# PEER routing in another place: heads routed at dots 1, 3 and 5, tile 1's first two heads together in group 7, and a reordered seam with banded pooling

## The chip, the cores and the metric

The kernel runs on one core of a Trainium2 chip. The time is the device time of the core in microseconds, the median of several executions; lower is better. The engines are PE (TensorE, matmuls), DVE (VectorE), ACT (ScalarE), POOL (GpSimd, here only an issuer of indirect gathers) and SP (SyncE, an issuer of plain transfers). Each works through its own list of instructions in order, and they wait for one another by semaphores.

## What is computed

The reference is a two-layer encoder over 256 tokens of width 2048 in float32. Layer 0 mixes with attention and an mLSTM, layer 1 with a multi-scale pooling:

```python
hn = rmsnorm(h, norm_mix_g[layer])
if layer % 2 == 0: h = h + attn_mlstm_mixer(hn, ...)
else:              h = h + multiscale_pool_mixer(hn, pool_w, layer_scale)
h = h + peer_ffn(rmsnorm(h, norm_ffn_g[layer]), peer_wq, peer_keys, peer_u, peer_v)
```

The pooling subtracts each token from the mean over a window of 2, 4, 8 or 16 tokens around it (a window for each of four channel groups), then applies a linear map for each group. Both layers end with a retrieval of experts (PEER, K = 16, 8 heads, 128 keys a side):

```python
q = (xn @ w_query).reshape(b, s, 8, 2, 128)
sc = einsum('bshpc,hpnc->bshpn', q, sub_keys)
s_top, i_top = top_k(sc, 16)                     # for each half of the key
cand = s_top[..., 0, :, None] + s_top[..., 1, None, :]
best, pos = top_k(cand, 16);  expert = i_top0 * 128 + i_top1 at pos
gate = softmax(best)
act = gelu(einsum('tkd,td->tk', u[expert], xt))  # 128 rows of u for each token
y   = einsum('tk,tkd->td', gate * act, v[expert])
```

## The kernel before

Tokens lie on the 128 partitions, in two tiles (t = 0, 1). In each layer the expert stage has 256 *rows*: row n gathers one expert vector of `u` for each of 128 tokens (a tile of 128 x 2048, 1 MB) and multiplies it with the token's normed input. Rows 0 to 127 belong to tile 0 and rows 128 to 255 to tile 1; sixteen rows are one head of one tile, a *group* (j = 0 to 15), and k counts the rows within a group.

*Gathers.* POOL issues them in the order of n (`gather_u`). At the first row of a group it waits for `idx_ready`, that is until DVE has written this group's indices into `idx_all`. Otherwise it waits for a free buffer: `U` has 6 slots for tile 0 (row n may go out when the dot six dots earlier is done), and the rows with n % 4 == 2 from group 1 to group 7 go to a second ring `UX` of 3, whose dot PE computes. For tile 1 `U` has 7 slots, the third row there waits until PE has done all of its dots (`ux_mm`), and the first until all routing is done, for the slots lie over the routing's buffers.

*DVE* runs through the rows: `dot(L, n)` for each row that isn't PE's, `pick` four times a group to read PE's results off a diagonal, and between the dots the routing, in three parts: `route_halves` (the 16 best of 128 scores on each side, with their indices, and the sums of pairs), `route_pairs` (the 16 best of 256), and `route`, which is `route_experts` (the indices, increments `idx_ready`) and `route_gates` (softmax, after an exponential on ACT). Ten *events* a layer go through one bank of PSUM with scores: tile 0 head 0, tile 0 head 1, tile 1 head 0, tile 1 head 1 (each for one tile), and heads 2 to 7 (each for both tiles). PE computes `queries` and `scores` of an event, ACT copies the queries (`route_q`), and `sc_free` keeps the scores of the next event off until DVE has read the last.

*PE* besides turns each `UX` row (`dot_u`: transposes, a copy by ACT in `turn_u`, and matmuls); the first row of a quad waits until the last quad's results are picked.

*SP* loads query weights `wq` into two slots by turns, a head's after PE has used the slot; then the weights of the dense part. Between the layers, at the *seam*, it loads the pooling matrices `PM`, `poolw`, the scale `lsB` (`PM` and `lsB` lie in the second `wq` slot), `wq` of head 0, the keys and the gains; `wq` of head 1 waits until the pooled result is added to `h` (`h1_ready`, 8). PE pools by full 128 x 256 matrices (L1629), though only the tokens within 8 of each other are not zero.

After the dots come the gathers of `v` (half of the width on DVE) and a dense part on PE; the change leaves them alone.

## Time and profile before

| | us |
|---|---|
| median of 3 runs | 3136.72 (3135.51 to 3137.5) |
| profiled execution | 3131.51 |
| its span, first to last instruction | 3129.6 |
| PE / DVE / ACT / POOL busy | 2292.8 / 2180.1 / 677.7 / 1011.0 |
| moved by the transfers | 1059.08 MB, mean 338 GB/s |
| mean granted clock of PE | 0.851 of 2.4 GHz |

The expert stage of layer 0 begins at 523.5 us of the span with the first gather, that of layer 1 at 1848.8. The seam is from 1782 to 1848. A row of a timeline says when an instruction (or a run of equal ones) began and how long it took, and in brackets how long its engine had been idle before it and who ended that. A busy engine that nobody waits for costs nothing, and an idle one costs only where its late work is waited for.

### The profile page before, as it was taken

What the parts mean: (1) busy time and instruction counts of PE and PEld (TensorE: products, weight loads), DVE (VectorE), ACT (ScalarE), POOL (GpSimd) and SP (SyncE); (2) the same over time, 40 slices, a digit from 0 to 9 for tenths busy, and PEclk for the clock granted to TensorE, in tenths of its full rate; (3) what the DMA queues carried; (4) which work ended last, traced back from release to release, by engine and by line L of the source; (5) the groups of instructions that cost most, each with busy time, mean ns of one, the idle gap of its engine ahead of it and who ended that gap; (6) DMA issues with size and microseconds to landing.
All of it is one profiled execution on the core that took longest, in us unless ns stands there. A gap on an engine that the chain in (4) does not pass through costs nothing.

```text
span 3129.6 us, 25966 instructions
## 1 busy us (share of the span) xinstructions
PE 2292.8 (73%) x9248; PEld 1706.4 (55%) x9248; DVE 2180.1 (70%) x3263; ACT 677.7 (22%) x1645; POOL 1011.0 (32%) x1028
## 2 busy tenths in 40 slices
PE   8999999588853400999999575888533109999994
PEld 4685545587743300766666344878533006666662
DVE  1341113988979999856666739889899998566667
ACT  1241111122229910200000011222289203000000
POOL 0000000432333333344544414233333333445444
PEclk9999999799975555999999787999855559999997
DMA  5423243989989999699999948899999996999998
GB/s 212 153 111 135 108 169 152 414 332 404 378 364 422 421 422 413 214 410 409 409 409 409 378 182 334 332 406 380 377 421 421 421 420 209 410 409 409 409 409 337
DMA packets 194528, 1059.08 MB, mean 338 GB/s; under 512 B 21856, under 2 KB 22240, under 8 KB 121312
## 3 DMA queue, kind: packets, MB, share of 16 engines
q0 software_dynamic: 147456, 805.37, 63.7%
q1 hardware_dynamic: 46944, 252.06, 20.3%
q8 instruction: 74, 1.21, 0.2%
q14 instruction: 54, 0.44, 0.0%
HBM read 1055.24 MB, written 2.10 MB: 338 GB/s over the span
## 4 chain that ended last, share of the span: by engine, by line
DMA 48%; PE 23%; DVE 22%; issue 3%; POOL 3%; ACT 1%; DVEq 0%; SPq 0%; ACTq 0%; POOLq 0%
DMA arena<-pu,idx_all 23%; DMA xnT<-pvg,idx_all 13%; DMA arena<-pvg,idx_all 11%; DVE arena L1120 10%; PE bank L1293 6%; DVE h L1146 4%; PE bank L1378 3%; PE bank L1599 2%; PE bank L1607 2%; PE low L1498 2%; PE bank L1533 1%; POOL arena L449 1%; PE low L1487 1%; PE low L1555 1%; PE bank L1487 1%
## 5 line engine op out<-in xcount | busy, mean ns | idle before, releaser
L1120 DVE CUSTOM_DVE_ANT_0 arena<-arena,low 128x2048 f32<-128x2048 f32 x420 | 954.2, 2286 | 125.1 <-DMA arena<-pu,idx_all 123.5
L449 POOL DMA_INDIRECT arena<-pu,idx_all x456 | 453.8, 995 | 1467.5 <-DVE idx_all L1094 767.3
L1616 PE MATMUL low<-arena 128*128 128x512 f32 x2048 | 879.6, 592 | 0.1
L1616 PEld LDWEIGHTS low<-arena 128*128 128x128 f32 x2048 | 604.7, 295 | 274.8 <-DMA arena<-pvd 1.0
L1146 DVE SCALAR_TENSOR_TENSOR h<-arena,cst,h 128x1024 f32<-128x1024 f32 x240 | 307.9, 1285 | 164.5 <-DMA arena<-pvg,idx_all 157.4
L1146 DVE SCALAR_TENSOR_TENSOR h<-xnT,cst,h 128x1024 f32<-128x1024 f32 x240 | 307.6, 1285 | 157.9 <-DMA xnT<-pvg,idx_all 150.9
L464 POOL DMA_INDIRECT arena<-pvg,idx_all x256 | 252.3, 986 | 296.8 <-DVE h L1146 215.7
L464 POOL DMA_INDIRECT xnT<-pvg,idx_all x256 | 250.3, 978 | 283.7 <-DVE h L1146 215.8
L1599 PE MATMUL bank<-arena 128*128 128x128 f32 x512 | 132.8, 441 | 201.6 <-ACT arena L728 201.6
L1533 PE MATMUL bank<-xnT,arena 128*128 128x256 f32 (+1 forms) x1280 | 239.2, 351 | 19.2 <-DMA arena<-wq 13.3
L1567 PE MATMUL bank<-xnT,arena 128*128 128x128 f32 x1792 | 247.6, 289 | 1.7 <-ACT arena L692 0.9
L497 ACT ACTIVATE arena<-h 128x2048 f32<-128x2048 f32 x10 | 19.1, 1905 | 1022.8 <-DVE h L1178 944.9
L1533 PEld LDWEIGHTS bank<-xnT,arena 128*128 128x128 f32 x1280 | 214.7, 203 | 42.0 <-DMA arena<-wq 14.1
L1567 PEld LDWEIGHTS bank<-xnT,arena 128*128 128x128 f32 x1792 | 233.1, 204 | 2.4 <-ACT arena L692 1.3
L1599 PEld LDWEIGHTS bank<-arena 128*128 128x128 f32 x512 | 114.0, 327 | 220.6 <-ACT arena L728 220.6
L1588 PE MATMUL bank<-cst,arena 128*128 128x128 f32 x8 | 2.8, 447 | 309.0 <-DVE cst L1135 309.0
L1293 PE MATMUL bank<-arena,xnT 128*128 128x512 f32 x448 | 198.7, 599 | 2.0 <-issue 1.6
L692 ACT ACTIVATE arena<-bank 128x512 f32<-128x512 f32 x224 | 133.8, 597 | 304.4 <-PE bank L1574 289.1
L1588 PEld LDWEIGHTS bank<-cst,arena 128*128 128x128 f32 x8 | 1.2, 204 | 310.0 <-DVE cst L1135 310.0
L1574 PE MATMUL bank<-cst,arena 128*128 128x128 f32 x608 | 103.3, 297 | 79.3 <-DVE cst L1129 25.8
L719 ACT ACTIVATE arena<-cst,arena 128x128 f32<-128x128 f32 x512 | 155.8, 389 | 0.1
L1293 PEld LDWEIGHTS bank<-arena,xnT 128*128 128x128 f32 x448 | 84.3, 192 | 101.8 <-issue 99.8
(222 smaller groups left out, 2218.8 us busy)
## 6 DMA issues: line engine op xcount, KB each, us to landing
arena<-pvd SPq DMA_DIRECT2D x256, 512.0 KB
arena<-w_proj SPq DMA_DIRECT2D x22, 2048.0 KB, 7.5
arena<-wq SPq DMA_DIRECT2D x16, 2048.0 KB
arena<-w_out SPq DMA_DIRECT2D x9, 2048.0 KB, 7.9
arena<-pu,idx_all POOLq DMA_INDIRECT x494, 14.8
gB<-gains SPq DMA_DIRECT2D x5, 1024.0 KB, 10.1
xnT<-pvg,idx_all POOLq DMA_INDIRECT x256
arena<-pvg,idx_all POOLq DMA_INDIRECT x256
```

Of the source, the lines that this page charges most:

```text
L449: nc.gpsimd.indirect_dma_start(U[t][slot], None, pu[L], bass.IndirectOffsetOnAxis(row(n), 0)).then_inc(u_got[t][slot], 16)
L464: nc.gpsimd.indirect_dma_start(vslots[m % VR], None, pvg[L], bass.IndirectOffsetOnAxis(idx_all[:, t * PH + hk // PK, hk % PK:hk % PK + 1], ...
L692: activation(UXT[i % 2][:, 4 * b:4 * b + 4], psum[4][:, :].rearrange("p (a b) -> p a b", a=4), ACT.Copy).then_inc(s["ux_ev"], 1)
L719: ins = activation(oh[:, b, i], iota, ACT.Square, scale=-1.0, bias=sT[:, x, t:t + 1])
L1120: vec.tensor_tensor_reduce(out=u, in0=u, in1=low[:, :] if staged else xns[t], scale=1.0, scalar=0.0, op0=ALU.mult, op1=ALU.add, accum_out= ...
L1146: vec.scalar_tensor_tensor(acc, vslots[m % VR], wv[:, t, hk:hk + 1], acc, ALU.mult, ALU.add).then_inc(s["vacc_done"], 1)
L1293: ins = mm(psum[4 + t][:, :], xnT[:, HALF * hf + k, t * P:(t + 1) * P], wslot[slot][:, k], start=hf == 0 and k == 0, stop=hf == 1 and k == ...
L1533: ins = mm(psum[6][:, p_ * S + t0 * P:p_ * S + t1 * P], wq_slots[slot][:, k, p_ * P:(p_ + 1) * P], xnT[:, k, t0 * P:t1 * P], start=k == 0, ...
L1567: ins = mm(psum[5][:, i % 4 * P:(i % 4 + 1) * P], UXT[i % 2][:, c], xnT[:, c, 0:P], start=c == 0, stop=c == KC - 1)
L1574: ins = tr(psum[4][:, x * P:(x + 1) * P], UX[i % UP][:, (4 * b + x) * P:(4 * b + x + 1) * P], ident)
L1599: ins = mm(psum[4 + q % 2][:, i * P:(i + 1) * P], o1[:, q % 2, i], o2[:, q % 2, i], start=True, stop=True)
L1616: ins = mm(psum[2 * t + c][:, 0:VH], W[t][:, :, n], vdense[:, n % DR, c * VH:(c + 1) * VH], start=n == 0, stop=n == NK - 1)
```

## The change

- Routing is counted by *routes* r = 0 to 8 (`ROUTES` = 9) beside the ten events of PE. Routes 0 and 1 are tile 0's heads 0 and 1; routes 2 to 7 are heads 2 to 7 of both tiles; route 8 is tile 1's heads 0 and 1 together, done in group 7.
- PE's events keep their order. The scores of tile 1's heads 0 and 1 are copied by ACT from PSUM to `keep` (`keep_scores`), which frees the bank without DVE.
- In groups 1 to 7 DVE has halves, pairs and experts after rows k = 1, 3 and 5 (group 1: 4, 5 and 7) and the gates after k = 9. In group 0 of layer 0 the whole of route 1 but its gates comes after k = 2, ahead of the mixer's add and the norm of tile 1; in layer 1 it is split to k = 4 and 6.
- In layer 1 ACT has the norm of tile 1 ahead of the copy of head 1's queries.
- `PM` and `lsB` lie elsewhere, and `wq` of head 1 is loaded without a wait, ahead of the gains.
- Pooling multiplies only the band of 136 columns (`BANDS`): for tile 0 one matmul, for tile 1 one of 16 and one of 120.

```diff
+BANDS = (((0, P + max(POOLW) // 2),), ((P - max(POOLW) // 2, P + max(POOLW) // 2), (P + max(POOLW) // 2, S)))
-EVENTS = PH + 2
+EVENTS, ROUTES = PH + 2, PH + 1
...
-        slot1 = wqb[:, 1].rearrange("p k c -> p (k c)")
-        PM = slot1[:, 0:D].rearrange("p (g t s) -> p g t s", g=4, t=TB)
-        lsB = slot1[:, D:2 * D]
+        carve = carver(OUT_AT + D, T_AT)
+        PM = carve(4, TB, S)
+        lsB = carve(D)
...
+                    load_wq(1, 1)
                     gain(3)
-                    sp.wait_ge(s["h1_ready"], 4 * TB)
-                    load_wq(1, 1)
...
-                    pool.wait_ge(s["idx_ready"], L * EVENTS + event(n // HK, n // PK % PH) + 1)
+                    pool.wait_ge(s["idx_ready"], ROUTES * (L + 1) if n // HK else ROUTES * L + n // PK + 1)
...
+            def keep_scores(L, hd):
+
+                e.wait_ge(s["sc_done"], EVENTS * L + hd + 3)
+                activation(keep[:, 2 * hd:2 * hd + 2], psum[7][:, 2 * P:4 * P].rearrange("p (a b) -> p a b", a=2), ACT.Copy
+                           ).then_inc(s["sc_free"], 1)
...
-                route_q(L, 1, 0, 1)
-                norm(1 + 2 * L, 1)
+                if L:
+                    norm(1 + 2 * L, 1)
+                    route_q(L, 1, 0, 1)
+                else:
+                    route_q(L, 1, 0, 1)
+                    norm(1 + 2 * L, 1)
                 evac_xt(1 + L, 1)
                 stage_xn(L, 0)
+                for hd in range(2):
+                    route_q(L, hd + 2, 1, 2)
+                    keep_scores(L, hd)
                 route_exp(L, 1, 0, 1)
-                for ev_ in (2, 3):
-                    route_q(L, ev_, 1, 2)
-                    route_exp(L, ev_, 1, 2)
                 route_q(L, 4, 0, 2)
...
+                if r == PH:
+                    v.wait_ge(s["sc_free"], EVENTS * L + 4)
+                    sc = keep
+                else:
+                    v.wait_ge(s["sc_done"], EVENTS * L + pe_event(r) + 1)
+                    sc = psum[7][:, :].rearrange("p (q n) -> p q n", q=4)
...
                         if j == 0:
-                            if k == (1 if L else 3):
-                                if L == 0:
-                                    add_mixer(1)
+                            if k == 3 and L == 0:
+                                add_mixer(1)
+                            if k == (1 if L else 4):
                                 norm(1 + 2 * L, 1)
-                            if k == (3 if L else 5):
+                            if k == (3 if L else 6):
                                 evac_xt(1 + L, 1)
-                            if k == 7:
+                            if k == (4 if L else 2):
                                 route_halves(L, 1, 0, 1)
-                            if k == 10:
+                            if k == (6 if L else 2):
                                 route_pairs(L, 1, 0, 1)
+                                route_experts(L, 1, 0, 1)
                             if k == 12:
-                                route(L, 1, 1, 0, 1)
...
+                                route_gates(L, 1, 0, 1)
+                        if 1 <= j < PH:
+                            if k == (4 if j == 1 else 1):
+                                route_halves(L, j + 1, 0, 2)
+                            if k == (5 if j == 1 else 3):
+                                route_pairs(L, j + 1, 0, 2)
+                            if k == (7 if j == 1 else 5):
+                                route_experts(L, j + 1, 0, 2)
                             if k == 9:
-                                route_pairs(L, 4, 0, 2)
-                            if k == 10:
-                                route(L, 2, 4, 0, 2)
-                        if 2 <= j < PH - 1:
-                            if k == 5:
-                                route_halves(L, j + 3, 0, 2)
-                            if k == 7:
-                                route_pairs(L, j + 3, 0, 2)
-                            if k == 9:
-                                route(L, j + 1, j + 3, 0, 2)
+                                route_gates(L, j + 1, 0, 2)
...
-                                ins = mm(psum[n][:, i * S:(i + 1) * S], xns[t][:, c * P:(c + 1) * P], PM[:, c // 4, t],
-                                         start=t == 0 and i == 0, stop=t == 1 and i == 1)
+                                for lo, hi in BANDS[t]:
+                                    ins = mm(psum[n][:, i * S + lo:i * S + hi], xns[t][:, c * P:(c + 1) * P],
+                                             PM[:, c // 4, t, lo:hi], start=t == 0 and i == 0, stop=i == 1 and hi == S)
```

SP's list at the seam, before: seven rows from the pooling matrix on.

```order
L393 DMA arena<-poolm 128x2048 [waits vacc_done,dense_done]
L394 DMA arena<-pool_w 128x8192
L395 DMA arena<-layer_scale 128x2048
L338 DMA arena<-wq 128x4096
L397 DMA arena<-keys 128x2048
L334 DMA gB<-gains 128x2048 [waits xn_ready]
L338 DMA arena<-wq 128x4096 [waits h1_ready]
```

The same place in the changed kernel:

```order
L395 DMA arena<-poolm 128x2048 [waits vacc_done,dense_done]
L396 DMA arena<-pool_w 128x8192
L397 DMA arena<-layer_scale 128x2048
L340 DMA arena<-wq 128x4096
L399 DMA arena<-keys 128x2048
L340 DMA arena<-wq 128x4096
L336 DMA gB<-gains 128x2048 [waits xn_ready]
```

The second `wq` (head 1) has lost its wait and stands ahead of the gains.

ACT's list at the start of layer 1's expert stage, before. L497 is the norm's square, L499 its root, L659 `route_q`, L665 `route_exp`, L505 the evacuation of the transposed input, L684 `stage_xn`.

```order
L659 ACTIVATE arena<-bank 128x2x128 [waits q_mm]
L497 ACTIVATE arena,stat<-h 128x2048 [waits pool_mm,h1_ready]
L499 ACT_TABLE_LOAD
L499 ACTIVATE stat<-stat 128x1 [waits ms_done]
L505 ACTIVATE xnT<-low 128x4x128 [waits tp_done] x2
L684 ACTIVATE low<-arena 128x512 [waits xt_dve,xt_act,xn_ready]
L684 ACTIVATE low<-arena 128x512 x3
L665 ACT_TABLE_LOAD
L665 ACTIVATE cst<-cst 128x16 [waits bd_ready]
L659 ACTIVATE arena<-bank 128x2x128 [waits q_mm]
L665 ACTIVATE cst<-cst 128x16 [waits bd_ready]
```

And after; L666 is `keep_scores`, L671 `route_exp`, L690 `stage_xn`:

```order
L497 ACTIVATE arena,stat<-h 128x2048 [waits pool_mm,h1_ready]
L499 ACT_TABLE_LOAD
L499 ACTIVATE stat<-stat 128x1 [waits ms_done]
L659 ACTIVATE arena<-bank 128x2x128 [waits q_mm]
L505 ACTIVATE xnT<-low 128x4x128 [waits tp_done] x2
L690 ACTIVATE low<-arena 128x512 [waits xt_dve,xt_act,xn_ready]
L690 ACTIVATE low<-arena 128x512 x3
L659 ACTIVATE arena<-bank 128x2x128 [waits q_mm]
L666 ACTIVATE arena<-bank 128x256 [waits sc_done]
L659 ACTIVATE arena<-bank 128x2x128 [waits q_mm]
L666 ACTIVATE arena<-bank 128x256 [waits sc_done]
L671 ACT_TABLE_LOAD
```

The norm has moved ahead of the query copy, and no exponential (with its wait for DVE, `bd_ready`) stands between the copies of tile 1's queries.

DVE's list in group 2, before: L1120 is a dot, L1129 a pick, L1036 the first and L1050 the last row of the halves, L1058 and L1074 of the pairs, L1084 and L1094 of the experts, L1105 the end of the gates.

```order
L1120 ISA arena,cst<-arena,low 128x2048
...
L1129 ISA arena,cst<-bank,cst 128x128
...
L1036 MAX arena<-bank 128x8 x4
...
L1050 TENSOR_TENSOR arena<-arena 128x256 x2
...
L1058 CAST arena<-i 128x64
...
L1074 TENSOR_TENSOR cst<-cst 128x32
...
L1084 TENSOR_SCALAR ab<-pos 128x2x16
...
L1094 SCALAR_TENSOR_TENSOR idx_all<-arena 128x2x16
...
L1105 TENSOR_TENSOR cst<-cst 128x2x16
```

And after, where L1150 is a pick, L1052 to L1069 the halves, L1076 to L1092 the pairs, L1101 to L1117 the experts, L1126 the end of the gates, L1141 a dot:

```order
L1052 MAX arena<-bank 128x8 x4
...
L1069 TENSOR_TENSOR arena<-arena 128x256 x2
...
L1150 ISA arena,cst<-bank,cst 128x128
...
L1076 CAST arena<-i 128x64
...
L1092 TENSOR_TENSOR cst<-cst 128x32
...
L1117 SCALAR_TENSOR_TENSOR idx_all<-arena 128x2x16
...
L1141 ISA arena,cst<-arena,low 128x2048
...
L1126 TENSOR_TENSOR cst<-cst 128x2x16
```

Before, the indices are written behind the dot of row k = 9, after the change behind that of row k = 5; the picks were ahead of the halves and now follow them; three dots stand between the experts and the gates.

## Rows read from the trace of the kernel before

**Rows 1.** The page: GB/s in 40 slices, and the chain's shares by engine.

```profile
GB/s 212 153 111 135 108 169 152 414 332 404 378 364 422 421 422 413 214 410 409 409 409 409 378 182 334 332 406 380 377 421 421 421 420 209 410 409 409 409 409 337
...
DMA 48%; PE 23%; DVE 22%; issue 3%; POOL 3%; ACT 1%; DVEq 0%; SPq 0%; ACTq 0%; POOLq 0%
```

**Rows 2.** Windows: length, busy time by engine, granted clock, transfer share, GB/s.

```profile
540.00:645.00 105.00, 65.93 (x379) 58.94 (x378) 92.82 (x223) 14.92 (x26) 39.24 (x30) 0.80 0.85 342
645.00:925.00 280.00, 223.07 (x1557) 206.38 (x1556) 248.64 (x513) 67.00 (x116) 89.96 (x96) 0.93 0.95 390
...
1850.00:1980.00 130.00, 76.35 (x448) 68.68 (x447) 103.60 (x234) 15.20 (x27) 45.03 (x33) 0.79 0.81 324
1980.00:2262.00 282.00, 226.19 (x1558) 209.58 (x1557) 249.77 (x513) 68.19 (x118) 91.50 (x98) 0.93 0.95 387
```

**Rows 3.** Timeline of POOL: its longest waits; row 4, then groups 2, 5, 7.

```profile
543.03 0.93 POOL L449 DMA_INDIRECT arena<-pu,idx_all  x1 [14.73 <-PE low L1498]
...
642.63 0.94 POOL L449 DMA_INDIRECT arena<-pu,idx_all  x1 [14.25 <-DVE idx_all L1094]
...
787.46 0.94 POOL L449 DMA_INDIRECT arena<-pu,idx_all  x1 [12.17 <-DVE idx_all L1094]
...
875.24 0.94 POOL L449 DMA_INDIRECT arena<-pu,idx_all  x1 [12.16 <-DVE idx_all L1094]
...
925.63 2.06 POOL L449 DMA_INDIRECT arena<-pu,idx_all  x1 [20.08 <-PE bank L1567]
...
1978.19 0.94 POOL L449 DMA_INDIRECT arena<-pu,idx_all  x1 [14.71 <-DVE idx_all L1094]
```

**Rows 4.** The chain that ended last, at the seam: start, length, what.

```profile
1789.65 6.68 PE low L1629 x16
1796.32 3.45 PE bank L1629 x16
...
1855.07 11.74 DMA arena<-wq
1866.85 9.29 PE bank L1533 x64
```

**Rows 5.** Timeline at the start of layer 1's expert stage.

```profile
1876.16 0.39 ACT L659 ACTIVATE arena<-bank 128x256 f32<-128x256 f32 x1 [30.29 <-PE bank L1533]
...
1878.47 0.15 DVE L803 TENSOR_SCALAR stat<-stat 128x1 f32<-128x1 f32 x1 [18.13 <-ACT arena L497]
...
1885.01 2.75 POOL L449 DMA_INDIRECT arena<-pu,idx_all  x1 [22.62 <-DVE cst L1120]
```

**Rows 6.** Timeline of DVE in layer 0: one-tile route, then two-tile route.

```profile
609.57 0.49 DVE L1036 MAX8 arena<-bank 128x8 f32<-128x128 f32 x2
...
612.79 2.29 DVE L1120 CUSTOM_DVE_ANT_0 arena<-arena,low 128x2048 f32<-128x2048 f32 x1
...
620.91 2.29 DVE L1120 CUSTOM_DVE_ANT_0 arena<-arena,low 128x2048 f32<-128x2048 f32 x1
...
765.86 0.89 DVE L1036 MAX8 arena<-bank 128x8 f32<-128x128 f32 x4
...
771.78 2.29 DVE L1120 CUSTOM_DVE_ANT_0 arena<-arena,low 128x2048 f32<-128x2048 f32 x1
...
778.28 2.28 DVE L1120 CUSTOM_DVE_ANT_0 arena<-arena,low 128x2048 f32<-128x2048 f32 x1
...
780.49 2.28 DVE L1120 CUSTOM_DVE_ANT_0 arena<-arena,low 128x2048 f32<-128x2048 f32 x1
...
787.74 2.29 DVE L1120 CUSTOM_DVE_ANT_0 arena<-arena,low 128x2048 f32<-128x2048 f32 x1
```

**Rows 7.** Timeline of PE in group 3: after the picks, queries, scores.

```profile
713.19 1.11 PE L1574 MATMUL bank<-cst,gB 128*128 128x128 f32 x4 [4.95 <-DVE cst L1129]
...
726.48 13.98 PE L1533 MATMUL bank<-xnT,arena 128*128 128x256 f32 x64
...
741.15 1.16 PE L1544 MATMUL bank<-arena 128*128 128x128 f32 x8 [0.69 <-ACT arena L659]
```

More of the change, by code:

```diff
@@ L58 @@
 VR, DR = 8, 4
+POOLW = (2, 4, 8, 16)
 HK = PH * PK
+BANDS = (((0, P + max(POOLW) // 2),), ((P - max(POOLW) // 2, P + max(POOLW) // 2), (P + max(POOLW) // 2, S)))
 ND, DG = 16, 2
@@ L134, in hybrid_encoder @@
         xn0 = carve(D)
+        keep = carve(4, NK)
         carve = carver(OUT_AT, T_AT)
@@ L274, in landed, with pe_event @@
             return 16 * (m // ring + 1)
-        def event(t, hd):
-            return 2 * t + hd if hd < 2 else hd + 2
+        def pe_event(r):
+            return r if r < 2 else r + 2
         class Steps:
@@ L1041, in route_halves @@
                     ins = vec.max_index(i16[:, q, 0:8], s16[:, q, 0:8], sc[:, q])
-                ins.then_inc(s["sc_free"], 1)
-                v.wait_ge(s["sc_free"], n0 + 1)
+                if r == PH:
+                    link(ins)
+                else:
+                    ins.then_inc(s["sc_free"], 1)
+                    v.wait_ge(s["sc_free"], EVENTS * L + pe_event(r) + 1)
                 for q in qs:
@@ L1186, in add_pooled @@
                     vec.tensor_tensor(h[:, t, cols], h[:, t, cols], ytmp[:, g % 2], ALU.add).then_inc(s["h1_ready"], 1)
-            def route(L, hd, ev_, t0, t1):
-                route_experts(L, hd, ev_, t0, t1)
-                route_gates(L, hd, ev_, t0, t1)
             add_mixer(0)
@@ L1208, in _ @@
                 route_pairs(L, 0, 0, 1)
-                route(L, 0, 0, 0, 1)
+                route_experts(L, 0, 0, 1)
+                route_gates(L, 0, 0, 1)
                 if L:
```

56 lines of the change are left out of this document (22 added, 34 removed).

## Prediction

> **What bounds the kernel now.** Read the chain first. Transfers hold 48% of it, PE and DVE less than a quarter each, and the largest part is the gather of `pu` rows [rows 1]. The line of rates beside it says the same in time: in the two gather stages the core moves 420 to 422 GB/s, and it never moves more. One gathered row (128 x 2048 floats, 1.049 MB) therefore costs 2.5 us of transfer and one head's query weights (2.1 MB) 5.0 us. Bytes are not changed much by this edit, so the question is how long the transfer engines stand idle.
>
> The windows give that. Each layer has 256 rows to gather; the first 128 (tile 0, groups 0 to 7) lie beside the routing, the other 128 run afterwards at the full rate. In the four windows of [rows 2] the rate is 342, 390, 324 and 387 GB/s. Against 420 that is 105 x 78/420 = 19.5 us lost at the start of layer 0, 280 x 30/420 = 20 us in its groups 2 to 7, 130 x 96/420 = 29.7 us at the start of layer 1, 282 x 33/420 = 22.2 us in its groups 2 to 7: 91 us in all. Nothing behind these stretches has slack against the gathers, so a microsecond of idle transfer removed there moves the end by one.
>
> Who makes it idle: [rows 3] are the issues of GpSimd (POOL) that waited longest. It stands before the first row of each group until `idx_all` of that group is written: 14.25 us at group 2, 12.17 us at group 5, 12.16 us at group 7, 14.71 us at group 2 of layer 1. From group 2 to 5 that is 144.8 us or 48.3 each, from 5 to 7 43.9 each. The last row of the list is another wait: row 130 needs all of PE's dots (20.08 us).
>
> In layer 1 a second hole comes first. The chain has a transfer of `wq` from 1855.07, 11.74 long, and PE's queries of head 1 behind it, 9.29 [rows 4]. ACT sat 30.29 us before copying these queries, and tile 1's norm stands behind that copy in ACT's queue; so DVE sat 18.13 us before the norm and POOL 22.62 us for a dot that stands behind the norm in DVE's queue [rows 5].
>
> **The change, part by part.** *Durations.* DVE's dots come every 2.21 us (778.28 to 780.49). A two-tile route is 5.92 (halves, 765.86 to 771.78), 6.50 less one dot = 4.29 (pairs, to 778.28) and 9.46 less two dots = 5.04 (experts with gates, to 787.74): 15.25 us. A one-tile route is 3.22 (609.57 to 612.79) and 8.12 less one dot = 5.91: 9.13 us [rows 6]. Four one-tile and six two-tile routes become two and seven: 128.0 against 125.0 us, 3 us less DVE work a layer. The two score copies on ACT are 256 columns, nearest the 0.39 us copy [rows 5], under 1 us in all; ACT is free there.
>
> *Start of layer 1.* `wq` of head 1 is issued with the seam's loads, `PM` and `lsB` having left its slot. Its 5.0 us of transfer goes where nothing moved, and the norm no longer stands behind the query copy. DVE's second dot ended at 1860.3 (1878.47 less 18.13) [rows 5]. I walk on from there: norm at 1861 to 1863, two dots and evacuation to 1869, one dot, halves of route 1 to 1874, two dots, pairs and experts to 1884. Group 1's indices are there before its rows are wanted. Tile 1's queries for heads 0 and 1 run on PE from 1869, about 9.3 each [rows 4], without DVE since scores are copied away; head 2's weights are asked for at 1878, and with 11.7 us as measured they land near 1890; its queries (14.0 [rows 7]) and scores are done by 1907, and DVE wants them at about 1913. DVE could then start group 2 near 1947. The transfers cannot: from 1851, 32 rows at 2.5 and three weights at 5 end at 1946, and I add 5 for two short gaps and the start: 1951 to 1953. Before, POOL released group 2 at 1978.19 [rows 3] and DVE reached it four dots later, at 1987. Gain 34 us, of which the idle share explains 29.7 and the moved weight 5.0. One rule of the Trainium skill bears on the 11.7: "DMA: Bandwidth & Descriptors", section "Queues, rings and completion order", says that each engine takes turns between its queues packet by packet, so a weight would get about half the rate beside gathers, 10 us for 2.1 MB. The row shows 11.74, so the trace agrees; by the page head 2's queries would start 2 us earlier and the sum stays.
>
> *Start of layer 0.* Here the order is the reverse: route 1 comes ahead of the mixer's add and the norm. POOL issues row 4 at 543.03 in both versions (it waits for PE) [rows 3]. Route 1 without gates (8.5 us) moves ahead of dot 3, so tile 1's norm is about 8 us later, near 557.6. Tile 1's queries follow to 572 and 582, head 2's from 585 to 602, scores at 603.5. ACT's exponential of route 1 stands behind both score copies, so DVE waits some 8 us at the gates (dot 12); that wait is hidden, since the scores of route 2 are not there before 603.5 anyhow and six rows are in flight. Then halves, dot, pairs, dot, experts, dot (22 us): group 2 is released at 625 and reached by DVE at 636. Transfers alone, 28 rows and three weights from 546, give 631. I take 639 for DVE. Before it was 642.63 + 9 = 652. Gain 13 us.
>
> *Groups 2 to 7.* Halves, pairs and experts now follow dots 1, 3 and 5 of a group, in place of 5, 7 and 9. Three clocks stand close together. Transfers: 16 x 2.5 = 40, or 45 where a weight is loaded (three of these groups). DVE: 12 x 2.21 + 15.25 + 0.85 for four picks = 42.6. PE: 13.3 for two turned rows (713.19 to 726.48), 14.0 queries, then scores ending at 742.3, 29.1 after the picks; two more turned rows and it can be picked again, 43 [rows 7]. Before, POOL issued nothing for 12.2 us in a stretch; after, the longest gaps are 7.4 us, twice, and six rows in flight are 15 us. So weight groups should fall from 48.3 to about 45.5, and plain ones stay at 43.5 to 43.9. A cost stands against this: the picks now come behind the halves, 5.9 us later in the group, PE runs later by as much, and POOL has to wait for PE at the second `UX` row of each group (to 48 us after the group's start, by 13.5 for the picks, 29.1 and 5.3 of turning, instead of 41). That wait fits into the backlog by my count. Gain 3 x 2.8 = 8 us.
>
> *Group 7.* It gets a whole route (15.25 us) which it did not have. DVE had only twelve dots and picks there, 27.4 us of the 50.4 from row 112 to row 130 [rows 3], so DVE fills up to 43. But row 126 can go out only after dot 7, 29.4 us into DVE's group, and row 130 waits for PE's dot of row 126; I make the release 45 to 46 us after DVE's group start, which in sum is 1 to 3 us worse than now. From DVE's group 2 to the release of row 130 it took 925.63 - 652 = 273.9 us; after, 267 (8 less 1 to 3). Layer 0: 652 - 639 + 6.5 = 19.5. Layer 1: 34 + 6.5 = 40.5.
>
> *Banded pooling.* 256 columns took 6.68 us for 16 passes at the low clock and 3.45 at the high one [rows 4]. The first tile's 136 columns save about 45%, roughly 2.5 to 3 us; the second tile's become two matmuls each with its own load of weights, 16 and 120 columns. Bounds for the 64 passes of tile 1: as wide as their columns 3.7 us, and as 128-column passes (9.29/64 = 0.145) 9.3, against 6.9 now. I take 7.4, so 2.4 us are gained. The Trainium skill speaks against this part: "TensorE: Matmul & The Clock Gate", section "LDWEIGHTS (loading the stationary operand)", gives P/1.2 ns for each load, an estimate of 107 ns by that page, so 64 passes could not take less than 6.8 us and tile 1 would gain nothing; the sum would be 0.6 us better than mine.
>
> **Sum.** 19.5 + 40.5 + 2.4 = 62.4. The profiled execution took 3131.5 us (span 3129.6 and 1.9 around it) and would become 3069; the median of the runs is 3136.7, 5.2 higher, so I predict 3136.7 - 62 = 3075.
>
> **Rivals.** (A) *All idle transfer goes.* 91 us is lost; the wait at row 130 (about 6.5 a layer) and the starts (7) stay, so at most 91 - 20 + 5 + 2.4 = 78: 3058. For it: GpSimd is free. Against: DVE and PE are each at 43 a group. (B) *The groups gain nothing*, because PE's later start and the blocked `UX` rows give back what the even spacing wins, or group 7 costs its full 5 us: only the starts count, 13 + 34 + 2.4 less up to 10: 39 to 49, near 3093. For it: the PE cycle of 43 has under 3 us of slack. (C) *Head 2's weights come late.* They are the first wait left at both starts. If they need 25 us beside the gathers in place of 11.7, DVE stands 13 us longer in layer 0 and 7 in layer 1: 3095. (D) *Slower.* PE falls to its low level within each group because it waits for the picks: after an idle of 4.95 us four passes took 1.11, where eight take 1.16 at 741.15 [rows 7]. At the low clock throughout, PE's 43 us becomes over 70. Twelve groups would have to lose over 5.2 us each beyond today's to use up 62; the time is then above 3137, with 3160 as the case's price (7 each). Against: in 645 to 925 the granted clock was 0.93 with waits of 5 us, and the change shortens these. (E) *The change does nothing*: the six dots in flight, not the indices, hold POOL. Against: the idle windows are empty of transfers while DVE works on routes.
>
> **Chances.** Forecast (3064 to 3086) 0.52; A 0.12; B 0.20; C 0.09; E, within 6 us of before, 0.03; D 0.04. A change of under 0.2% (6 us) is what a measurement of this kernel cannot tell. Faster 0.93, same 0.03, slower 0.04. The range takes in A and most of B and C: 3055 to 3101.
>
> **What would show it.** In layer 1 no DVE wait of 18 us before the norm and no stretch without transfers near 1876 to 1890; POOL's waits for `idx_all` inside the groups gone or under 3 us, its waits for PE before `UX` rows grown to 5 or more; group pitch near 45.5 and 43.7; row 130 released near 906 and 2218; DVE waiting some 8 us at the gates of route 1 in layer 0. It is wrong if the pitch in groups 2 to 7 stays at 48, or if group 2 of layer 1 is released later than 1960.

## The result and the profile after

| | before | changed | forecast |
|---|---|---|---|
| median, us | 3136.1 (4 runs, 3131.8 to 3137.5) | 3061.4 (4 runs, 3057.6 to 3062.4) | 3075 (3055 to 3101) |
| ratio | 1 | 0.9762 (0.9745 to 0.9779) | 0.980 |
| span of the profiled execution | 3129.6 | 3055.8 | |

The kernel is 74.7 us faster. Direction and range hold; the gain is 12 us larger than the forecast's 62.4. A second set of runs of the same changed kernel (first experiment below) gave 3061.13 and a span of 3058.9, so both executions are shown where stages are compared.

The page of the changed kernel, the line of rates and the chain's shares, which answer to [rows 1]:

```profile
GB/s 211 143 125 140 116 110 198 358 421 420 403 380 422 421 422 418 208 410 409 409 409 409 372 215 423 416 421 393 392 421 422 422 412 216 410 409 409 409 409 331
...
DMA 46%; PE 25%; DVE 24%; issue 3%; POOL 1%; ACT 1%; DVEq 0%; SPq 0%; ACTq 0%; POOLq 0%
```

Where the line read 414, 332, 404, 378, 364 in layer 0 and 334, 332, 406, 380, 377 in layer 1, it now reads 358, 421, 420, 403, 380 and 423, 416, 421, 393, 392. The slices are a little shorter than before, and the first of layer 0's (358) takes in the slow start of its first group; behind it both gather stages move 380 to 423 GB/s beside the routing. The windows, cut at the corresponding places of the new trace, answer to [rows 2]:

```profile
540.00:640.00 100.00, 72.60 (x419) 64.07 (x418) 85.01 (x148) 17.15 (x29) 44.35 (x34) 0.85 0.95 388
640.00:901.00 261.00, 211.73 (x1519) 197.79 (x1516) 248.57 (x562) 64.01 (x112) 87.18 (x93) 0.93 1.00 407
1822.00:1928.00 106.00, 81.81 (x522) 72.78 (x520) 94.18 (x167) 19.07 (x33) 49.90 (x39) 0.90 1.00 409
1928.00:2188.00 260.00, 207.67 (x1484) 194.00 (x1484) 250.84 (x564) 62.48 (x110) 87.97 (x93) 0.93 1.00 407
```

342, 390, 324 and 387 GB/s have become 388, 407, 409 and 407. The idle transfer that is left is 7.6, 8.1, 2.8 and 8.0 us (window times 32/420, 13/420, 11/420, 13/420), 26 in place of 91. That is 65 us less; with the 5 us of the weight load that now moves in the seam it is 70, and the four windows are 70 us shorter in sum (727 for 797).

The list of waits, first two rows of POOL and the DVE row (engine, what it works on, whom it waits for, us in total, times, longest):

```profile
POOL arena L449 <- DVE cst L1141: 702.8, 363, 7.4
POOL arena L449 <- DVE idx_all L1117: 597.5, 2, 523.0
...
DVE arena L1141 <- DMA arena<-pu,idx_all: 82.1, 252, 6.9
```

Before, POOL waited 16 times for indices; two of these are left, the first gathers of the two layers. Its longest wait for a buffer that DVE gives back fell from 22.6 to 7.4 us (8.4 in the second execution). The timeline of POOL shows what it waits for now, against [rows 3]:

```profile
641.84 0.94 POOL L428 DMA_INDIRECT gB<-pu,idx_all  x1 [4.29 <-PE bank L1580]
...
780.32 0.94 POOL L428 DMA_INDIRECT gB<-pu,idx_all  x1 [6.71 <-PE bank L1580]
...
884.81 0.95 POOL L428 DMA_INDIRECT arena<-pu,idx_all  x1 [0.30 <-issue]
...
900.76 0.94 POOL L449 DMA_INDIRECT arena<-pu,idx_all  x1 [7.11 <-PE bank L1573]
1821.26 0.94 POOL L449 DMA_INDIRECT arena<-pu,idx_all  x1 [74.44 <-DVE idx_all L1117]
...
2187.58 0.94 POOL L449 DMA_INDIRECT arena<-pu,idx_all  x1 [7.11 <-PE bank L1573]
```

900.76 and 2187.58 are the releases of row 130 (925.63 and 2260.83 before). The stages between such marks say where the 74 us came from. "Group 2" is the DVE dot that opens it, at 638.47 and 1928.49 in the changed kernel.

| stage | before | changed, two executions | gain | forecast |
|---|---|---|---|---|
| layer 0: row 4 issued to DVE at group 2 | 108.7 | 95.5, 99.0 | 13.3, 9.7 | 13 |
| layer 0: DVE at group 2 to release of row 130 | 273.9 | 262.3, 257.5 | 11.6, 16.4 | 6.5 |
| from there to the first gather of layer 1 | 923.1 | 920.5, 921.5 | 2.6, 1.6 | 2.4 |
| layer 1: first gather to DVE at group 2 | 138.5 | 107.2, 109.5 | 31.3, 29.0 | 34 |
| layer 1: DVE at group 2 to release of row 130 | 273.5 | 259.1, 259.1 | 14.4, 14.4 | 6.5 |

Starts and seam came out as forecast within the 2 to 5 us by which two executions differ. The second and the last row together gave 26 to 31 us where 13 were forecast. There the 12 us lie.

### The profile page after: what moved, and what is told of

The parts are those of the page before. It is cut to its first block, busy times and chain, and to the rows that moved or that the text cites. A ratio compares the mean times of both kernels' runs of the same rounds, so it can differ in the third digit from the quotient of the medians.

```text
span 3055.8 us, 26007 instructions
## 1 busy us (share of the span) xinstructions
PE 2271.4 (74%) x9280; PEld 1691.7 (55%) x9280; DVE 2173.0 (71%) x3241; ACT 678.1 (22%) x1647; POOL 1010.2 (33%) x1028
## 4 chain that ended last, share of the span: by engine, by line
DMA 46%; PE 25%; DVE 24%; issue 3%; POOL 1%; ACT 1%; DVEq 0%; SPq 0%; ACTq 0%; POOLq 0%
DMA xnT<-pvg,idx_all 23%; DMA arena<-pu,idx_all 20%; DVE arena L1141 11%; PE bank L1299 6%; DVE h L1167 4%; PE bank L1384 3%; PE bank L1539 2%; DMA arena<-pvg,idx_all 2%; PE bank L1605 2%; PE bank L1613 2%; PE bank L1573 2%; PE low L1504 1%; PE low L1493 1%; PE bank L1493 1%; PE bank L1580 1%
## 5 line engine op out<-in xcount | busy, mean ns | idle before, releaser
L1141 DVE CUSTOM_DVE_ANT_0 arena<-arena,low 128x2048 f32<-128x2048 f32 x420 | 951.9, 2286 | 74.2 <-DMA arena<-pu,idx_all 73.0
L497 ACT ACTIVATE arena<-h 128x2048 f32<-128x2048 f32 x10 | 19.1, 1907 | 1041.2 <-DVE h L1199 945.7
L1573 PEld LDWEIGHTS bank<-xnT,arena 128*128 128x128 f32 x1792 | 228.8, 201 | 0.0
L1539 PEld LDWEIGHTS bank<-xnT,arena 128*128 128x128 f32 x1280 | 208.7, 196 | 32.8 <-issue 8.5
```

Of the source, the lines that this page charges most:

```text
L1141: vec.tensor_tensor_reduce(out=u, in0=u, in1=low[:, :] if staged else xns[t], scale=1.0, scalar=0.0, op0=ALU.mult, op1=ALU.add, accum_out= ...
L1539: ins = mm(psum[6][:, p_ * S + t0 * P:p_ * S + t1 * P], wq_slots[slot][:, k, p_ * P:(p_ + 1) * P], xnT[:, k, t0 * P:t1 * P], start=k == 0, ...
L1573: ins = mm(psum[5][:, i % 4 * P:(i % 4 + 1) * P], UXT[i % 2][:, c], xnT[:, c, 0:P], start=c == 0, stop=c == KC - 1)
```

## The experiments

All edits start from the changed kernel, except where the text says otherwise. Each median is of 4 or 5 executions, and the kernel before was run beside each of the four sets (3134.1, 3136.4, 3136.8 and 3137.3). Executions of one kernel spread by 2 to 13 us, so a difference of 3 or 4 us is at the edge of what these medians tell.

**The changed kernel again.**

> The changed kernel once more, as the reference of this series. Both theories: a span of 3056 us, 74 below that of the kernel before, row 130 released at 901 and 2188 us.

3061.13 us (3056.9 to 3062.9), ratio 0.9763 (0.9747 to 0.9779).

**The order at the seam, whole and in parts.** First both the weight load and ACT's order go back to what they were, then ACT's order alone, then the load alone.

```diff
-                    load_wq(1, 1)
                     gain(3)
+                    sp.wait_ge(s["h1_ready"], 4 * TB)
+                    load_wq(1, 1)
...
-                if L:
-                    norm(1 + 2 * L, 1)
-                    route_q(L, 1, 0, 1)
-                else:
-                    route_q(L, 1, 0, 1)
-                    norm(1 + 2 * L, 1)
+                route_q(L, 1, 0, 1)
+                norm(1 + 2 * L, 1)
```

> Of the changed kernel only the two edits at the seam are undone: head 1's query weights wait for the pooled sum again and stand behind the gains, and ACT copies the queries ahead of tile 1's norm. Theory 1 (the hole at the start of layer 1 was made by these two together, and its transfers count in full): DVE waits 18 us before the norm again, transfers stand idle for 14 us, and 5 us of weights move back beside the gathers: 19 us longer than the changed kernel. Theory 2 (the early indices of group 1 and the copied scores would have closed the hole in any case, because six more rows could be in flight): under 5 us longer.

> Only the order on ACT is undone (query copy ahead of tile 1's norm); the weights are early. Theory 1: PE's queries of head 1 end at 1833.5, so the norm comes some 4 us later and most of that is hidden: 0 to 4 us longer than the changed kernel. If the order on ACT were the cause of the hole and not the late weights: 15 us or more.

> Only the load of head 1's weights is undone (waits for the pooled sum, behind the gains); ACT has the norm first. Theory 1: 5 us of transfer beside the gathers, and tile 1's transposes stand behind PE's queries of head 1, so DVE waits at the evacuation: 5 to 15 us longer. If the order on ACT were the cause of the hole: only the 5 us of transfer.

Both undone: 3078.17 us, ratio 0.9818 (0.9801 to 0.9834), 17 slower than the changed kernel. ACT's order alone: 3065.06, 0.9775 (0.9758 to 0.9791), 4 slower, with an interval that overlaps the changed kernel's. The load alone: 3069.69, 0.9799 (0.9782 to 0.9816), 8.6 slower. Timeline of layer 1's start with both undone (the window ends inside PE's run of 64 matmuls, here and in the next block):

```profile
1842.60 2.71 PE L1536 MATMUL bank<-xnT,arena 128*128 128x128 f32 x11 [13.29 <-DMA arena<-wq]
...
1852.39 0.38 ACT L660 ACTIVATE arena<-bank 128x256 f32<-128x256 f32 x1 [30.81 <-PE bank L1536]
...
1854.70 0.15 DVE L809 TENSOR_SCALAR stat<-stat 128x1 f32<-128x1 f32 x1 [17.80 <-ACT arena L498]
...
1861.24 2.75 POOL L450 DMA_INDIRECT arena<-pu,idx_all  x1 [23.13 <-DVE cst L1138]
```

This is [rows 5] again, nearly to the digit: ACT 30.8, DVE 17.8, POOL 23.1 us. With the load late but the norm ahead of the copy:

```profile
1841.34 3.99 PE L1540 MATMUL bank<-xnT,arena 128*128 128x128 f32 x17 [13.15 <-DMA arena<-wq]
...
1852.78 0.69 DVE L827 COPY xnT<-low 128x512 f32<-128x512 f32 x1 [7.91 <-PE low L1288]
```

PE stands just as long, but DVE passes the norm and is caught only at the transposed input, 7.9 us in place of 17.8. With the weights early and only ACT's order old, DVE waits 2.2 us before the norm. Either half of the edit removes more than half of the stall, and only the two together all of it: 4 and 8.6 undone singly, 17 jointly.

**Routing at dots 5, 7, 9 again,** group 7 still with its route.

```diff
-                            if k == (4 if j == 1 else 1):
+                            if k == (4 if j == 1 else 5):
                                 route_halves(L, j + 1, 0, 2)
-                            if k == (5 if j == 1 else 3):
+                            if k == (5 if j == 1 else 7):
                                 route_pairs(L, j + 1, 0, 2)
-                            if k == (7 if j == 1 else 5):
+                            if k == (7 if j == 1 else 9):
                                 route_experts(L, j + 1, 0, 2)
```

> Of the changed kernel only the places in groups 2 to 7 are undone: halves, pairs and experts of a route after dots 5, 7 and 9 in place of 1, 3 and 5. Theory 1 (the even spacing lets gathers go out in the stretch where all stood before the indices): groups with query weights go back from about 45 to 48 us, and row 128 waits for the indices of group 7: 8 us a layer, 12 to 20 us longer than the changed kernel. Theory 2 (the spacing gives nothing, the gain in groups 2 to 7 comes from the removed one-tile routes and from copied scores): under 3 us.

3089.70 us, ratio 0.9851 (0.9832 to 0.9871): 28 slower than the changed kernel, more than the 12 to 20 expected. The waits of [rows 3] are back, six a layer, the last of them at row 128, since tile 1's first heads are now routed in group 7:

```profile
910.82 0.94 POOL L449 DMA_INDIRECT arena<-pu,idx_all  x1 [12.23 <-DVE idx_all L1117]
...
2170.89 0.94 POOL L449 DMA_INDIRECT arena<-pu,idx_all  x1 [12.17 <-DVE idx_all L1117]
2214.78 0.94 POOL L449 DMA_INDIRECT arena<-pu,idx_all  x1 [12.23 <-DVE idx_all L1117]
```

From DVE's group 2 to row 130 it took 274.9 and 272.2 us, the old kernel's times, while the two starts (98.4 and 109.0) stayed the changed kernel's. So the place of the routes alone carries the second and fifth row of the table. It is their place and not a more even spacing: at 5, 7 and 9 the three parts stand as far apart as at 1, 3 and 5, but POOL wants the next group's indices before the last part has written them, and then stands through two parts in one stretch.

**Group 0 of layer 0 in its old order** (norm at k = 3, copies at 5, route 1 at 7 and 10), and **ACT's exponential of route 1 ahead of the two score copies.** Both ask whether the arrangement in layer 0's start counts.

```diff
-                            if k == (4 if L else 2):
+                            if k == (4 if L else 7):
                                 route_halves(L, 1, 0, 1)
-                            if k == (6 if L else 2):
+                            if k == (6 if L else 10):
```

> Only group 0 of layer 0 goes back to the old order: the mixer's add and the norm after dot 3, evacuation after 5, halves of route 1 after 7, pairs and experts after 10. Theory 1: group 1's indices are some 6 us late for its first row, but tile 1's queries come 8 us sooner; of the 13 us gained at the start of layer 0 most came from the copied scores and the missing one-tile routes, so 0 to 6 us longer. Theory 2 (route 1 ahead of the norm made the 13 us): 10 us or more longer.

```diff
+                if L == 0:
+                    route_exp(L, 1, 0, 1)
                 for hd in range(2):
                     route_q(L, hd + 2, 1, 2)
                     keep_scores(L, hd)
-                route_exp(L, 1, 0, 1)
+                if L:
+                    route_exp(L, 1, 0, 1)
```

> In layer 0 ACT has the exponential of route 1 ahead of the copies of tile 1's queries and scores, so DVE's wait of 7.5 us at the gates goes. Theory 1 (that wait is hidden by the rows in flight and by the later scores): same time as the changed kernel within 2 us, and a longer DVE wait for data or scores in group 1. Theory 2: 5 to 7 us shorter.

3061.09 (0.9761, 0.9745 to 0.9778) and 3061.94 (0.9766, 0.975 to 0.9783): neither differs from the changed kernel. With the exponential first, DVE has no wait at the gates, and waits for gathered rows instead: 3.58, 3.24 and 2.65 us at the dots from 584 to 595, where the changed kernel has 0.15 and 2.02.

**Pooling over all 256 columns,** all else as changed.

```diff
-BANDS = (((0, P + max(POOLW) // 2),), ((P - max(POOLW) // 2, P + max(POOLW) // 2), (P + max(POOLW) // 2, S)))
+BANDS = (((0, S),), ((0, S),))
```

> Only the pooling goes back to full 128 x 256 matrices. Both theories of the size: PE's pooling takes 17.1 us from its first matmul in place of 13.5. My count said 2.4 us for the seam, the seam as a whole got 1.1 shorter: 1 to 3 us longer, within the noise of the total, to be read from the seam's rows.

3062.14, ratio 0.9769 (0.9753 to 0.9785), no difference the median can tell. In the trace the stretch from row 130 to layer 1's first gather is 922.4 us against 920.5 and 921.5. The chain at the seam, first with the band (the changed kernel), then without:

```profile
1763.21 3.96 PE low L1636 x16
1767.18 2.51 PE bank L1636 x16
1769.68 3.56 PE low L1636 x32
1773.25 3.57 PE bank L1636 x32
...
1801.81 9.36 PE bank L1539 x64
```

```profile
1764.75 6.68 PE low L1636 x16
1771.43 3.45 PE bank L1636 x16
1774.88 3.45 PE low L1636 x16
1778.33 3.45 PE bank L1636 x16
...
1806.39 7.39 PE bank L1539 x64
```

The band saves 3.4 us of pooling (17.0 to 13.6), all in tile 0: 10.1 to 6.5, while tile 1's passes go from 6.9 to 7.1. Then head 0's queries of layer 1, which stand behind the pooled add and the norm, take 9.36 us where they take 7.39 without the band (7.40 in the kernel before). Windows over those queries, band first:

```profile
1801.00:1812.00 11.00, 9.72 (x67) 9.56 (x68) 0.60 (x1) 0.79 (x2) 0.00 (x0) 0.78 0.01 1
```

```profile
1806.00:1814.00 8.00, 7.38 (x64) 7.22 (x64) 0.18 (x1) 0.19 (x1) 0.00 (x0) 1.00 0.01 2
```

The granted clock is 0.78 with the band and 1.00 without: part of these queries ran at the low level (1.2 GHz). That takes 2.0 of the 3.4 us back. From the first pooling matmul to the end of these queries it is 48.0 us with the band and 49.0 without, a gain of 1.1.

The traces of the other experiments hold eleven more executions with the band. In ten of them the queries took 9.0 to 9.6 us at a granted clock of 0.76 to 0.82. In one, the run with both seam edits undone, they took 7.38 at 1.00, and there tile 0's pooling had already been quicker (5.4 us, where the others took 5.7 to 6.9), with a granted clock of 0.88 over the pooling where the others had 0.79 to 0.86. So the band goes with slow queries without making them certain; what decides it was not tested.

**The place of the picks.** In the changed kernel POOL waits 4.0 to 6.7 us for PE at a `UX` row in eight of the twelve groups (five in the second execution). If PE's late start costs time, earlier picks should win it.

```diff
-                        if 2 <= j <= PH and k == 3:
+                        if 2 <= j <= PH and k == 1:
```

> The changed kernel (about 3061 us) with the four picks of groups 2 to 8 after dot 1 and ahead of the halves, in place of after dot 3. Halves (5.9 us) and two dots (4.4) then no longer stand ahead of them, so PE starts up to 10 us earlier in a group and POOL's waits for PE at the second UX row (4.0 to 6.7 us in the changed kernel) shrink by as much. My theory says these waits lie in the backlog of six issued rows: the time stays within 5 us of 3061, with waits under 2 us. The rival (the forecast's PE clock is the tightest of the three, and each of the 12 groups loses 1 us or more to it) says 3040 to 3052. A third outcome: the routes move by 1 us of picks and the waits for the indices return; then over 3066.

3083.11, ratio 0.9837 (0.982 to 0.9853): 22 slower, against both theories. The third outcome has the time right (over 3066) but not the cause, for POOL waits for buffers and not for indices. DVE's and POOL's timeline in layer 1's group 3:

```profile
1993.32 0.29 DVE L1150 CUSTOM_DVE_ANT_0 arena<-bank,cst 128x128 f32<-128x128 f32 x1 [6.37 <-PE bank L1573]
```

```profile
2002.67 0.94 POOL L449 DMA_INDIRECT arena<-pu,idx_all  x1 [10.12 <-DVE cst L1141]
```

The pick reads the last quad's results, and after dot 1 PE hasn't finished them. DVE stands 6.4 us, the dots behind it give their buffers back late, and POOL issues nothing for 10.1 us in a stretch. A pick waits for PE as much as PE waits for it. (The picks moved by 8.1 us, the halves and one dot; k = 2 is PE's row, so the 10 us of the expectation counted a dot too many.) With the picks behind the halves, one dot earlier than in the changed kernel:

```diff
-                        if 2 <= j <= PH and k == 3:
+                        if 2 <= j <= PH and k == 2:
```

> The changed kernel with the four picks of groups 2 to 8 after dot 2, one dot (2.2 us) earlier, between the changed kernel's place (after dot 3) and the one before the halves that cost 22 us. There DVE waited 2.5 to 6.7 us at the picks for PE's dots of the group's earlier rows, and POOL then up to 10.1 us for a buffer; in the changed kernel it waits 0 to 1.3 us. Theory (the place of the picks is right where PE has just finished, and before that every microsecond is lost on DVE): DVE waits 1 to 4 us at the picks of the weight groups, POOL's waits for PE before the UX rows fall by about 2 us, and the time is 3062 to 3070. Rival (PE's start is what the groups wait for, and only the wide misplacement hurts): no waits over 1.5 us at the picks and 3050 to 3058.

3062.05, ratio 0.9759 (0.9746 to 0.9773): no difference. DVE waits at three picks, 1.5 to 2.0 us, and POOL's waits of over 4 us for PE at `UX` rows are two, of 4.1, in place of the five and eight of the changed kernel's two executions. But these had waits at the picks too, up to 1.3 and 2.05 us, so the two arrangements hardly differ there. The rival's 3050 to 3058 is out: fewer waits for PE gave nothing. Two microseconds at the picks are swallowed; six are not.

**Group 7's route late in its group** (halves after dot 7, pairs 8, experts 9, gates 11).

```diff
-                            if k == (4 if j == 1 else 1):
+                            if k == (4 if j == 1 else 7 if j == PH - 1 else 1):
...
-                            if k == (7 if j == 1 else 5):
+                            if k == (7 if j == 1 else 9 if j == PH - 1 else 5):
```

> The changed kernel with the route of group 7 (heads 0 and 1 of tile 1) later in its group: halves after dot 7, pairs after 8, experts after 9, gates after 11. In the changed kernel row 126 went out 23.65 us after DVE's group start and row 130 39.6 us after it, with 7.1 us of waiting for PE. If row 126's place behind the routing is what delays row 130, then here it goes out about 10 us earlier; but row 128 is the first that wants the indices, which come about 10 us later (some 31 us after the group start instead of 21). My theory says the two offset each other within 4 us of 3061: row 128 and row 129 wait for indices instead of row 130 for PE. The rival (row 130's wait for PE costs its full 7.1 us a layer and can be had back) says 3050 or less.

3064.87, ratio 0.9776 (0.9759 to 0.9792), 3.5 to 3.7 slower than the two sets of the changed kernel. POOL's timeline at the end of group 7, layer 0:

```profile
875.18 0.94 POOL L428 DMA_INDIRECT arena<-pu,idx_all  x1 [0.30 <-issue]
...
896.82 0.94 POOL L449 DMA_INDIRECT arena<-pu,idx_all  x1 [18.10 <-DVE idx_all L1117]
...
904.07 0.94 POOL L449 DMA_INDIRECT arena<-pu,idx_all  x1 [5.08 <-PE bank L1573]
```

Row 126 goes out 13.5 us after DVE's group start instead of 23.7, but row 128 waits 18.1 for its indices; row 130 comes at 42.4 instead of 39.6 to 40.7. Moving this route later doesn't win the wait for PE back.

**No kept scores:** the kernel before with all the rest of the change, tile 1's heads 0 and 1 as two one-tile routes in group 1 again, and no route in group 7. Against the changed kernel:

```diff
-                for hd in range(2):
-                    route_q(L, hd + 2, 1, 2)
-                    keep_scores(L, hd)
                 route_exp(L, 1, 0, 1)
+                for ev_ in (2, 3):
+                    route_q(L, ev_, 1, 2)
+                    route_exp(L, ev_, 1, 2)
...
+                        if j == 1:
+                            for hd in range(2):
+                                if k == 3 * hd + 1:
+                                    route_halves(L, hd + 2, 1, 2)
+                                if k == 3 * hd + 2:
+                                    route_pairs(L, hd + 2, 1, 2)
+                                if k == 3 * hd + 3:
+                                    route(L, hd, hd + 2, 1, 2)
```

> The changed kernel without kept scores: tile 1's heads 0 and 1 are again routed as two one-tile routes after dots 1 to 3 and 4 to 6 of group 1, head 2 after 8 to 10, and group 7 has no route; the seam's order, the banded pooling, the early route 1 of group 0, and dots 1, 3, 5 in the other groups are as changed. Group 1 then has 33.5 us of routing in place of 15.3, and group 2's rows are released about 18 us later in each layer; the group 7 without its 15.3 us gives back up to 10 a layer. Theory: moving that work is worth 20 to 26 us of the 75, so 3081 to 3087. Rival (the order of the seam and the even spacing do it all): under 3066. A third: group 7 gives nothing back, then 3090 to 3097.

3088.54, ratio 0.9848 (0.9831 to 0.9864): 27 slower, just above the theory's 3081 to 3087 and below the third outcome. Layer 0, POOL's timeline:

```profile
645.86 0.94 POOL L449 DMA_INDIRECT arena<-pu,idx_all  x1 [14.66 <-DVE idx_all L1098]
...
914.30 1.95 POOL L449 DMA_INDIRECT arena<-pu,idx_all  x1 [20.96 <-PE bank L1574]
```

DVE reaches group 2 at 109.5 us after row 4 (108.7 before, 95.5 and 99.0 changed), and in layer 1 at 120.1 after the first gather (107.2 and 109.5). In group 7, row 130 is released 40.3 and 40.4 us after DVE's group start, as in the changed kernel with its whole route there. So a route in group 7 costs nothing: PE's dots set this release, and DVE's 15 us fit beside them.

## Why the prediction was right, and by how much it was off

**What bounds the kernel, and the 91 us of idle transfer: right.** The changed kernel gained 74 and leaves 26 by the same count. What was undone one part at a time adds up: 17 (seam order), 28 (place of the routes), 27 (kept scores), about 1 (pooling) and 0 (layer 0's inner order) make 73 of 74.7.

**Start of layer 1: mechanism right, 34 forecast, 29 to 31 measured.** The seam's order (127.7 us in this stage with both its parts undone, so 18 to 21) and the kept scores (120.1, so 11 to 13) make it up. There is no long wait at the norm any more, and the timeline has the norm at 1833.9. Head 2's weights, asked for at 1849.4, were there after 10.2 us:

```profile
1859.62 14.08 PE L1539 MATMUL bank<-xnT,arena 128*128 128x256 f32 x64 [0.75 <-DMA arena<-wq]
```

Rival C (weights after 25 us) is out: the twelve weight loads beside gathers took 10.2 to 12.8 us. From the rule in the Trainium skill's "DMA: Bandwidth & Descriptors", section "Queues, rings and completion order", that an engine takes turns between its queues, an estimate is half of the 420 GB/s, or 10 us. The trace agrees with it as a lower end: 10.2 is the quickest of the twelve, and 11.74 of [rows 4] lies in their middle.

The 3 to 5 us that are missing from the forecast's 34 are bytes and not gaps. From the first gather to DVE's group 2 the transfers moved 407 GB/s over 107.2 us (398 over 109.5 in the second execution), 43.6 MB, which against 420 is 3.3 and 5.7 us of idle, about the 5 that I added. But I counted 32 rows and three weights, 39.8 MB, or 95 us. By that time a fourth weight (asked for at 1919.0) and rows beyond row 32 had been moving too, and the 43.6 MB take 104.

**Start of layer 0: number right (13 forecast; 13.3 and 9.7), reasons half right.** The wait at the gates was forecast at some 8 us and called hidden:

```profile
583.78 0.17 DVE L1124 TENSOR_REDUCE cst<-cst 128x1 f32<-128x16 f32 x1 [7.50 <-ACT cst L671]
```

It is 7.5 and, as its removal showed, costs nothing. But the walk through group 0 suggested that route 1's early place has a part in the 13 us. It has none: the old order gives the same time, and without kept scores the whole 13 is gone. The gain is the routing taken out of group 1.

**Groups 2 to 7: the term that was mis-sized.** I wrote "weight groups should fall from 48.3 to about 45.5, and plain ones stay at 43.5 to 43.9. ... Gain 3 x 2.8 = 8 us". From DVE's group 2 to group 7, five groups, took 232.6 and 233.1 us before, 222.7 and 219.5 in the changed kernel, 216.8 and 217.9 in its second execution. That is 10 to 16 us a layer, on the mean 13.6. The step that failed is taking the largest of three clocks group by group. Five groups carry 80 rows (200 us of transfer) and three weights (15): 215 in all, 43.0 on the mean. The six rows in flight carry a weight's 5 us over into the next group, which needs only 40. My pitches add up to 223.9, as though each plain group had to stand at 43.7 whatever the transfers had in hand. Measured were 44.3 us on the mean for the first three of the five groups (nine of twelve under the 45 that a weight group's bytes take) and 43.2 for the last two. The windows over 220 us of layer 0, before and in the second execution of the changed kernel, show the same stretch fuller:

```profile
640.00:860.00 220.00, 186.54 (x1286) 171.62 (x1285) 198.65 (x443) 51.69 (x89) 74.02 (x79) 0.97 0.94 384
```

```profile
640.00:860.00 220.00, 182.18 (x1303) 168.31 (x1302) 212.06 (x471) 53.16 (x93) 76.15 (x82) 0.98 1.01 416
```

Over the five groups themselves the same bytes moved before and after (90.2 MB, and 89.8 to 91.3), at 387 and 388 GB/s before and at 409 to 416 now. DVE's own clock, 42.6, is reached in many groups of both layers and is now as tight as the transfers. No run took the weights out of these groups, so that the backlog carries them over is read from these rows and not tested by itself.

**Group 7: forecast 45 to 46 us from DVE's group start to row 130, measured 39.6 in both layers** (second execution 40.7 and 41.1; before 41.3 and 40.4). The step "row 126 can go out only after dot 7, 29.4 us" was wrong. Row 126 takes a `UX` slot and needs no dot of DVE; it stands only behind row 125 in POOL's queue, which needs the dot six dots earlier, k = 5. It was issued at 884.81, 23.7 after the group start:

```profile
861.16 2.28 DVE L1141 CUSTOM_DVE_ANT_0 arena<-arena,low 128x2048 f32<-128x2048 f32 x1
```

The "1 to 3 us worse" of this group was on the mean 0.6 better, and the run without the route shows the route itself at nothing. The groups (+5.6 a layer on the mean) and group 7 (+2) make more than the 12 us; the starts give some back.

**Pooling: 2.4 forecast, about 1 measured, by another sum.** I took 7.4 us for tile 1 between bounds of 3.7 and 9.3, and 7.13 were measured, 0.2 more than before. The Trainium skill's page "TensorE: Matmul & The Clock Gate", section "LDWEIGHTS (loading the stationary operand)", gives P/1.2 ns for a load, by that page an estimate of 107 ns for 128 columns, so that tile 1 could gain nothing. The trace agrees: 64 passes in 7.13 us are 111 ns each, and my lower bound of 3.7 us would be 58. Tile 0 gave 3.7, more than forecast, and the clock of the queries took 2.0 of it back, which no rival had.

**Other signs.** POOL's waits for indices inside the groups are gone, and its waits for PE before `UX` rows have grown to 4.0 to 6.7, the first as forecast, the second near the forecast 5 or more. Row 130 of layer 0 came at 900.8 for 906. For layer 1 I wrote 2218, which leaves out layer 0's gain; by my own sum it is 2198, and 2187.6 was measured. Rival A (all idle goes, 3058) came nearest in size, and its reason, that the transfers and not DVE or PE set the pace, fits groups 2 to 7 better than my sum did; the idle time that it left was 20 us, and 26 were measured. B (the groups gain nothing) is refuted by the 28 us of the run with the old places. D (a slower clock) is out, the granted clock in the groups stayed at 0.93; E (no effect) is out by 74.7 us. The test with early picks shows how near a rival of B's kind stood: the same work with the picks 8.1 us earlier gives 22 of the 75 us back.

**Open.** Single groups still take 47.1 us in some executions and 42.6 in others. The 47.1 are DVE's 42.6 and one wait for a gathered row, in group 4 of both layers of the first execution; in layer 0 it is

```profile
734.12 2.29 DVE L1141 CUSTOM_DVE_ANT_0 arena<-arena,low 128x2048 f32<-128x2048 f32 x1 [4.41 <-DMA arena<-pu,idx_all]
```

The weight load asked for at 723.8 was under way then (12.8 us). In the second execution the same load, asked for at 727.3, delayed no row, and the group took 42.6: there the backlog had room for it. What tips a group into the one or the other was not tested. That the seam's two halves cost 17 together and 12.6 apart rests on the timelines shown, and was not taken further.

## What to carry to other kernels

When transfers with a backlog are the bound, add their work over several groups before comparing it with the engines' clocks; the maximum of each group overstates the sum, here 223.9 against 216.8 to 222.7 measured, with bytes for 215. Work whose result another engine's queue waits for is best placed before that queue wants it: the same routing in the same groups, in parts equally far apart, cost 28 us when it stood four rows later, because POOL then issued nothing for 12 us at each group's first row. Where two engines hand results to each other in a ring, find the time at which the other has just finished before moving a hand-over: 8.1 us too early cost 22 us, 2.2 us too early nothing.

## What the runs showed of the hardware

- Shorter work ahead can go with slower work behind: with the pooling cut by 3.4 us, queries 25 us later had a granted clock of 0.78 in place of 1.00 and took 9.36 us for 7.39. The order of everything between was the same, with PE idle for 6.6 us before the transposes that lead up to them. Eleven of twelve executions with the shorter pooling show it, one (7.38 us at 1.00) does not.
- Splitting 32 matmuls of 256 columns into 64 of 16 and 120 columns, little over half the columns, took them from 6.9 to 7.1 us: 111 ns a matmul, on the mean of the two widths.
- The twelve plain 2 MB transfers beside the gathers landed after 10.2 to 12.8 us. While the quickest was under way (1849.4 to 1859.6) the core moved 420 GB/s in all, no more than the gathers alone, and the 2.1 MB of the load in 10.2 us are 206 of these: it had about half.
